# Two-layer decoder trunk on one core: the first weight tile loaded in two parts, and the blocks for the down-projection sums read ahead of two pooling weights

## The chip, the core and the metric

The kernel runs on one core of a Trainium2 chip. The metric is the device time of one execution in microseconds. The core has five engines with instruction streams of their own: TensorE (PE; weight loads show as PEld), VectorE (DVE), ScalarE (ACT), GpSimd (POOL) and SyncE (SP). SP does no arithmetic here: it issues most DMAs, in the order of its own program, and one that must wait holds up all that stand behind it. Engines tell each other of finished work by semaphores only.

## What is computed

Two layers over a stream x of 1024 positions by 1024 features, all in float32. Layer 0, cut to the parts that lie around the change:

```python
h = rms_norm(x, norm_gains[0, 0])
z = h @ w_in[0]                                  # 1024 x 1024
z_main, z_mem = z[..., :768], z[..., 768:]
y_main = pool_mixer(z_main, w_pool[0], pool_scale[0])   # causal means over 2/4/8/16 positions, then a product
y_mem = memory_attn(z_mem, mem, mem_norm[0], w_mem_kv[0])   # 4 heads over 256 memory rows
y = jnp.concatenate([y_main, y_mem], axis=-1) @ w_out[0]
x = x + rms_norm(y, norm_gains[0, 1])
h = rms_norm(x, norm_gains[0, 2])
gu = h @ w_gate_up[0]
y = (silu(gu[..., :2816]) * gu[..., 2816:]) @ w_down[0]
x = x + rms_norm(y, norm_gains[0, 3])
```

After layer 0 a shared K/V is projected; layer 1 has dilated attention in place of the pooling mixer and is otherwise built alike.

## The kernel before

**Tiling.** Features lie on the 128 partitions and positions along the free axis. A weight job is one 128-column tile of a weight matrix, 8 tiles of 128 x 128 (8 x 64 KB, 512 KB), or 3 of them (192 KB) for a pooling weight. Every float32 operand is split into a rounded high part and the rest as low part, and a product is three matmuls (high x high, high x low, low x high). For weights ACT makes the high part (WH from WR, `weight_hi`, L1076) and DVE or POOL the low part (WL, L1719 on DVE, L2599 on POOL). A job on 1024 positions is 6 matmuls of 512 columns for each of its k tiles.

**Start.** SP loads the constants (CN, 121 KB), the gains (GN, 47 KB), weight job 0, x tiles 0 to 3 (XS, 512 KB each, in two DMAs), weight job 1, x tiles 4 to 7. Of each x tile ACT makes the high part (XHA, L1234) and DVE the low part (XLA, `x0_low`, L1738). In between ACT and DVE split weight 0 (ahead of x tile 0) and weight 1 (ACT behind x tile 5, DVE behind x tile 6). PE runs job 0 ("in" tile 6) and waits before each k for `x0_lo`.

**Pooling stage (about 152 to 213 us).** Jobs 12 to 17 are the products with the pooling weights, in the order of POOL_OUT. In each job PE runs two attention steps of the memory heads in between. A step of PE is: PO (probabilities times values, L837), PTR (transpose of the probabilities, L847), PSC (scores, L865). A step of DVE is: maximum of the scores (MC, L1862), its negative (NM, L1868), and for the step before the reciprocal and scaling (RL L1881, PR L1882). ACT does the exponential (PR, L1191) and the copy of the transposed probabilities (PT, L1185). They hand over in a ring, so a wait of one holds all three. After the steps of job n ACT takes the product out of PSUM (YP, L1284) and splits coming weights: one for n = 0 and 1, two for n = 2 and 3, always the next ones in the list.

**Sums of the down-projection weights.** The down projection is a fast matrix product with 7 products, and needs sums of blocks of w_down. For each of 8 block sets c, SP reads two DMAs of 704 KB into ZS[c % 2] (`load_blocks`, L2773), DVE makes four sums in place (`weight_sums`, L1966 to L1970) and SP writes them back (`keep_blocks`, L2781). ZS[0] and ZS[1] lie on the memory of XLA, so set 0 may be read only when the last "in" job (job 11) is done. DVE makes the sums of set 0 around the two steps of pooling job 13 (n = 1; L1966 and L1967 ahead of the first step), those of sets 1 and 2 in n = 3 and 4, the others in the output projection.

**SP around this stage.** A weight may be read when the job that last used its slot is done. Slots go round in fours: the weight of job 15 waits for job 11, of job 16 for job 12, of job 17 for job 13. Output weights 0 to 3 (called out 0 to out 3 here; WR4 to WR7) lie on the memory of XS, and are free. SP's order is: weights 15, 16, 17, out 0 to out 3, block sets 0 and 1, then for each set: write it back, and read the one after next once this write has landed.

Of the kernel before, what the change touches and what calls it, by code (L numbers as in the profile page):

```python
# [10 lines left out]
ALU = mybir.AluOpType  # L11
# [3 lines left out]
P = 128  # L15
# [285 lines left out]
def build(nc, w_all, w_st, w_dn, x_t, mem_t, pos, gains, consts, masks, x_mid, inner, mem_keep, rstd_keep,  # L301
          trig_keep, w_keep, s_keep, t_keep, out_t):
    with ExitStack() as ctx:
# [210 lines left out]
        consts_in, tables_in = sem("consts_in"), sem("tables_in")  # L514
# [166 lines left out]

        px_order = {"PE": [], "ACT": []}
# [5 lines left out]
        def _(pe):  # L688
# [9 lines left out]
            def begin(j):  # L698

                pe.wait_ge(*lo_ready(j))  # L700
                for s, v in dict.fromkeys(PS_WAIT[j].values()):
                    pe.wait_ge(named[s], v)
# [175 lines left out]
            pe.wait_ge(consts_in, 32)  # L878

            xh, xl = xs(0)  # L880
            job(J[("in", 0, 6, None)], xh, xl, wait_k=lambda k: pe.wait_ge(x0_lo, k + 1))
# [182 lines left out]
        def _(act):  # L1064
# [164 lines left out]
            act.wait_ge(consts_in, 32)  # L1229
            A(NM[:, :], CN[:, 0:2], ACT.Copy)  # L1230
            weight_hi(0)
            for k in range(KT):
                act.wait_ge(x_in[k], 32)
                A(XHA[:, :, k, :], XS[:, k, :].rearrange("p (h c) -> p h c", h=2), ACT.Copy,  # L1234
                  scale=GN[:, k:k + 1]).then_inc(x0_hi, 1)
                if k == 5:
                    weight_hi(1)
            weight_hi(2)
# [464 lines left out]
        def _(dve):  # L1703
# [195 lines left out]
            dve.wait_ge(consts_in, 32)  # L1899
            weight_lo(J[("in", 0, 6, None)])  # L1900
            for k in range(KT):
                x0_low(k)
                if k == 6:
                    weight_lo(J[("in", 0, 7, None)])
            for k in range(1, KT):
                accumulate0(k)
            memory_low()
# [669 lines left out]
        def _(pool):  # L2577
# [32 lines left out]
            pool.wait_ge(consts_in, 32)  # L2610
# [84 lines left out]
        def _(sp):  # L2695
            loaded = [0]

            def load(j):
# [22 lines left out]
                sp.dma_start(raw(j), src.rearrange("p (k n) -> p k n", k=o.kn)).then_inc(s, 16)  # L2721
# [142 lines left out]
            def sub_layer(l):  # L2864

                if l == 0:
                    loads_to(J[("out", 0, 4, 0)])
                    sp.wait_ge(mm_done, J[("in", 0, POOL_IN[-1], None)] + 1)
                    load_blocks(0, 0)
                    load_blocks(0, 1)  # L2870
                    for c in range(8):
# [40 lines left out]
            sp.dma_start(CN[:, :], consts).then_inc(consts_in, 16)  # L2912
            sp.dma_start(GN[:, :], gains).then_inc(consts_in, 16)
            loads_to(1)
            for k in range(KT):
                if k == 4:
                    loads_to(2)
# [10 lines left out]
            loads_to(J[("out", 0, 0, 0)])  # L2928
# [139 lines left out]
```

## Time and profile before

| | us |
|---|---|
| Median of 3 runs | 2176.41 |
| Lowest and highest of them | 2172.22, 2179.36 |
| The profiled execution's own time | 2175.9 |
| Its span, first to last instruction | 2174.1 |
| PE busy | 2080.0 (96%) |
| DVE, ACT, POOL busy | 1474.5, 955.0, 338.2 |
| DMA, mean over the span | 164 GB/s |

The span is cut by what PE does: its busy time is 96% of it. The rest, 94 us, is made of waits, most of them shorter than 3 us. Busy times of matmuls are modelled, so starts are better read than ends. Times of a row count from the start of the span.

### The profile page before, as it was taken

To read this page: it belongs to the slowest core of one execution; us is meant where nothing else is said; L and a number is where in the kernel's file an instruction comes from. 1 tells how busy PE (TensorE), PEld (TensorE's weight loads), DVE (VectorE), ACT (ScalarE), POOL (GpSimd) and SP (SyncE) were. 2 spreads that over 40 slices of the span, in tenths; PEclk is the share of its full clock that TensorE was granted. 3 is DMA by queue.
4 is the path that set the end of the run, shared out by engine and by line. 5 is a ranking of instruction groups with operands and counts; after the bars stand their busy time and mean duration, and the time that the engine had idled before them with its cause. 6 is when DMAs were issued, how large, how long until landed. Compare 5 with 4: busy or idle time off the path is not lost.

```text
span 2174.1 us, 25430 instructions
## 1 busy us (share of the span) xinstructions
PE 2080.0 (96%) x9458; PEld 1676.4 (77%) x9458; DVE 1474.5 (68%) x2079; ACT 955.0 (44%) x1513; POOL 338.2 (16%) x188
## 2 busy tenths in 40 slices
PE   7995899999999999999999998999999999999997
PEld 6774788788888888887777776678788888877886
DVE  5555678477788875575455466467969998885665
ACT  6333354355554354343445556665622222234441
POOL 3632200021121000000000023020033333310001
PEclk9998999999999999999999999899999999999998
DMA  4206842355678876574111100113236654477554
GB/s 168 93 15 223 296 157 83 117 180 225 232 271 303 307 275 218 193 281 160 59 59 59 59 30 30 39 54 117 82 134 219 245 206 158 172 266 259 191 185 154
DMA packets 119755, 357.37 MB, mean 164 GB/s; under 512 B 10832, under 2 KB 12112, under 8 KB 114384
## 3 DMA queue, kind: packets, MB, share of 16 engines
q1 hardware_dynamic: 103168, 325.59, 42.0%
q10 hardware_dynamic: 16464, 30.15, 4.0%
q8 instruction: 75, 1.23, 0.2%
q14 instruction: 48, 0.39, 0.1%
HBM read 241.28 MB, written 114.43 MB: 164 GB/s over the span
## 4 chain that ended last, share of the span: by engine, by line
PE 73%; DVE 9%; DMA 7%; ACT 5%; issue 4%; SPq 1%; POOL 0%; ACTq 0%; POOLq 0%; DVEq 0%
PE PS L941 10%; PE PS L943 10%; PE PS L942 10%; PE PS L716 7%; PE PS L721 7%; PE PS L717 6%; PE PS L959 5%; PE PS L960 5%; PE PS L961 5%; PE PSC L865 3%; PE PO L837 2%; PE PTR L847 1%; DMA TP<-x_mid 1%; DVE SS L1754 1%; DMA inner<-TP 1%
## 5 line engine op out<-in xcount | busy, mean ns | idle before, releaser
L959 PE MATMUL PS<-RP,DH 128*128 128x512 f32 x616 | 241.0, 391 | 5.1 <-DVE RP L2181 5.1
L960 PE MATMUL PS<-RP,DH 128*128 128x512 f32 x616 | 239.8, 389 | 0.0
L961 PE MATMUL PS<-RP,DL 128*128 128x512 f32 x616 | 239.8, 389 | 0.0
L941 PE MATMUL PS<-BHT,SH 128*128 128x512 f32 x576 | 224.1, 389 | 0.0
L942 PE MATMUL PS<-BLT,SH 128*128 128x512 f32 x576 | 224.1, 389 | 0.0
L943 PE MATMUL PS<-BHT,SL 128*128 128x512 f32 x576 | 224.1, 389 | 0.0
L941 PE MATMUL PS<-BH,SH 128*128 128x512 f32 x432 | 168.2, 389 | 0.7 <-DVE SL L2082 0.7
L943 PE MATMUL PS<-BH,SL 128*128 128x512 f32 x432 | 168.1, 389 | 0.0
L942 PE MATMUL PS<-BL,SH 128*128 128x512 f32 x432 | 168.0, 389 | 0.0
L959 PEld LDWEIGHTS PS<-RP,DH 128*128 128x128 f32 x616 | 115.6, 188 | 31.4 <-DVE RP L2181 7.5
L1076 ACT ACTIVATE DH<-DR 128x1408 fp32r<-128x1408 f32 x56 | 77.3, 1380 | 135.5 <-DMA DR<-s_keep 88.5
L961 PEld LDWEIGHTS PS<-RP,DL 128*128 128x128 f32 x616 | 115.6, 188 | 24.3
L960 PEld LDWEIGHTS PS<-RP,DH 128*128 128x128 f32 x616 | 115.7, 188 | 23.5
L716 PE MATMUL PS<-XH,WH 128*128 128x512 f32 x320 | 132.4, 414 | 0.8 <-ACT TP L1604 0.4
L1191 ACT ACTIVATE PR<-PSC,NM 128x256 f32<-128x256 f32 (+1 forms) x144 | 63.4, 440 | 145.2 <-DVE NM L1868 144.8
L1335 ACT ACTIVATE SH<-SR 128x2048 fp32r<-128x2048 f32 x36 | 69.1, 1920 | 130.5 <-POOL SR L2680 94.4
L717 PE MATMUL PS<-XL,WH 128*128 128x512 f32 x320 | 126.0, 394 | 0.0
L943 PEld LDWEIGHTS PS<-BHT,SL 128*128 128x128 f32 x576 | 108.1, 188 | 22.6
L942 PEld LDWEIGHTS PS<-BLT,SH 128*128 128x128 f32 x576 | 108.1, 188 | 22.4
L941 PEld LDWEIGHTS PS<-BHT,SH 128*128 128x128 f32 x576 | 108.1, 188 | 22.3
L2645 POOL TENSOR_TENSOR VL<-VR,VH 128x1024 fp32r<-128x1024 f32 x24 | 58.2, 2423 | 416.1 <-ACT VH L1218 416.1
L1719 DVE TENSOR_TENSOR DL<-DR,DH 128x1408 fp32r<-128x1408 f32 x56 | 90.5, 1621 | 40.4 <-ACT DH L1076 40.3
(327 smaller groups left out, 4830.0 us busy)
## 6 DMA issues: line engine op xcount, KB each, us to landing
SR<-in_wst SPq DMA_DIRECT2D x36, 1024.0 KB, 4.8
ZS<-in_wdn SPq DMA_DIRECT2D x32, 704.0 KB, 5.8
s_keep<-ZS SPq DMA_DIRECT2D x32, 704.0 KB, 4.7
DR<-s_keep SPq DMA_DIRECT2D x32, 704.0 KB, 5.2
WR<-in_w SPq DMA_DIRECT2D x36, 512.0 KB, 4.8
inner<-TP SPq DMA_DIRECT2D x36, 512.0 KB, 4.4
DR<-in_wdn SPq DMA_DIRECT2D x24, 704.0 KB, 5.4
RR<-t_keep SPq DMA_DIRECT2D x16, 1024.0 KB, 5.2
```

Source lines behind the costliest of these rows:

```text
L716: MM(out[h], wh[:, i, :], rh(h, k), start=(i == 0), stop=False)
L717: MM(out[h], wh[:, i, :], rl(h, k), start=False, stop=False)
L721: ins = MM(out[h], wl[:, i, :], rh(h, k), start=False, stop=last)
L941: MM(BANK[bank], SH[b][:, w, c], BH[t][:, k, :], start=(k == 0), stop=False)
L942: MM(BANK[bank], SH[b][:, w, c], BL[t][:, k, :], start=False, stop=False)
L943: ins = MM(BANK[bank], SL[b][:, w, c], BH[t][:, k, :], start=False, stop=(k == 3))
L959: MM(bank, wh[:, i, :], rh, start=(i == 0), stop=False)
L960: MM(bank, wh[:, i, :], rl, start=False, stop=False)
L961: ins = MM(bank, wl[:, i, :], rh, start=False, stop=(i == KD - 1))
L1076: A(hi(j), raw(j), ACT.Copy).then_inc(w_hi, 1)
L1335: A(SH[pair_slot(q)][:, S3:, :], SR[pair_slot(q)][:, S3:, :], ACT.Copy).then_inc(st_hi, 1)
L1719: V.tensor_tensor(lo(j), raw(j), as_f32(hi(j)), ALU.subtract).then_inc(w_lo_dve, 1)
```

## The change

Two edits, both in layer 0.

1. **Start.** SP loads the gains first, then the first two k tiles of weight 0 (128 KB), x tile 0, the other six k tiles (384 KB), x tiles 1 to 3, then the constants, weight 1 and x tiles 4 to 7. ACT and DVE split weight 0 in two parts, around x tile 0. PE waits for the first part at k = 0 and for the second at k = 2. The waits for the constants are moved behind this on all engines.
2. **Block sets.** After the weight of job 15 SP waits for job 11 and reads sets 0 and 1; then weight 16, write-back of set 0, weight 17, read of set 2, and only then out 0 to out 3. From the write-back of set 1 on its order is as before.

No arithmetic is added; splitting weight 0 makes one DMA, one ACT and one DVE instruction more.

```diff
 PE
             def begin(j):
-                pe.wait_ge(*lo_ready(j))
+                if j:
+                    pe.wait_ge(*lo_ready(j))
...
-            pe.wait_ge(consts_in, 32)
+            def first_ready(k):
+                if k == 0:
+                    pe.wait_ge(first_lo, 1)
+                elif k == K0:
+                    pe.wait_ge(*lo_ready(0))
+                pe.wait_ge(x0_lo, k + 1)
...
-            job(J[("in", 0, 6, None)], xh, xl, wait_k=lambda k: pe.wait_ge(x0_lo, k + 1))
+            job(J[("in", 0, 6, None)], xh, xl, wait_k=first_ready)
+            pe.wait_ge(consts_in, 16)
 ACT
-            act.wait_ge(consts_in, 32)
-            A(NM[:, :], CN[:, 0:2], ACT.Copy)
-            weight_hi(0)
+            act.wait_ge(gains_in, 16)
+            A(NM[:, :], GN[:, 0:2], ACT.Copy)
+            act.wait_ge(first_in, 16)
+            A(hi(0)[:, 0:K0, :], raw(0)[:, 0:K0, :], ACT.Copy).then_inc(first_hi, 1)
+            hi_next[0] += 1
             for k in range(KT):
+                if k == 1:
+                    act.wait_ge(*load_seen(0))
+                    A(hi(0)[:, K0:, :], raw(0)[:, K0:, :], ACT.Copy).then_inc(w_hi, 1)
...
+            act.wait_ge(consts_in, 16)
             weight_hi(2)
 DVE
-            dve.wait_ge(consts_in, 32)
-            weight_lo(J[("in", 0, 6, None)])
+            dve.wait_ge(gains_in, 16)
+            dve.wait_ge(first_hi, 1)
+            V.tensor_tensor(lo(0)[:, 0:K0, :], raw(0)[:, 0:K0, :], as_f32(hi(0)[:, 0:K0, :]),
+                            ALU.subtract).then_inc(first_lo, 1)
+            lo_next[0] += 1
             for k in range(KT):
+                if k == 1:
+                    dve.wait_ge(w_hi, 1)
+                    V.tensor_tensor(lo(0)[:, K0:, :], raw(0)[:, K0:, :], as_f32(hi(0)[:, K0:, :]),
+                                    ALU.subtract).then_inc(w_lo_dve, 1)
                 x0_low(k)
...
             for k in range(1, KT):
                 accumulate0(k)
+            dve.wait_ge(consts_in, 16)
 SP
                 if l == 0:
                     loads_to(J[("out", 0, 4, 0)])
-                    sp.wait_ge(mm_done, J[("in", 0, POOL_IN[-1], None)] + 1)
-                    load_blocks(0, 0)
-                    load_blocks(0, 1)
-                    for c in range(8):
+                    for c in range(1, 8):
                         keep_blocks(0, c)
...
-            sp.dma_start(CN[:, :], consts).then_inc(consts_in, 16)
-            sp.dma_start(GN[:, :], gains).then_inc(consts_in, 16)
-            loads_to(1)
+            sp.dma_start(GN[:, :], gains).then_inc(gains_in, 16)
+            sp.dma_start(raw(0)[:, 0:K0, :], w_all[ROW["in", 0, 6], :, 0:K0 * P].rearrange("p (k n) -> p k n", k=K0)) \
+                .then_inc(first_in, 16)
             for k in range(KT):
+                if k == 1:
+                    loads_to(1)
                 if k == 4:
+                    sp.dma_start(CN[:, :], consts).then_inc(consts_in, 16)
                     loads_to(2)
...
-            loads_to(J[("out", 0, 0, 0)])
+            loads_to(J[("pool", 0, POOL_OUT[4], None)])
+            sp.wait_ge(mm_done, J[("in", 0, POOL_IN[-1], None)] + 1)
+            load_blocks(0, 0)
+            load_blocks(0, 1)
+            load(J[("pool", 0, POOL_OUT[4], None)])
+            keep_blocks(0, 0)
+            load(J[("pool", 0, POOL_OUT[5], None)])
+            load_blocks(0, 2)
             sp.wait_ge(x0_lo, KT)
             sub_layer(0)
```

`load` with j = 0 leaves out the first K0 = 2 k tiles, and POOL waits for `gains_in` and `consts_in` in place of the one count.

SP's order in the pooling stage before. WR3, WR0 and WR1 with 384 columns are the weights of jobs 15, 16 and 17, WR4 to WR7 are out 0 to out 3, ZS0 and ZS1 the block sets (x2: two DMAs):

```order
L2721 DMA WR3_116<-in_w 128x384
L2721 DMA WR0_113<-in_w 128x384
L2721 DMA WR1_114<-in_w 128x384
L2721 DMA WR4_117<-in_w 128x1024
L2721 DMA WR5_118<-in_w 128x1024
L2721 DMA WR6_119<-in_w 128x1024
L2721 DMA WR7_120<-in_w 128x1024
L2773 DMA ZS0_253<-in_wdn 128x2x704 x2
L2773 DMA ZS1_254<-in_wdn 128x2x704 x2
L2781 DMA s_keep<-ZS0_253 128x2x704 x2
L2773 DMA ZS0_253<-in_wdn 128x2x704 x2
```

And SP's order there now (L2749 is the weight load, L2801 the block read, L2809 the write-back):

```order
L2749 DMA WR3_116<-in_w 128x384
L2801 DMA ZS0_253<-in_wdn 128x2x704 x2
L2801 DMA ZS1_254<-in_wdn 128x2x704 x2
L2749 DMA WR0_113<-in_w 128x384
L2809 DMA s_keep<-ZS0_253 128x2x704 x2
L2749 DMA WR1_114<-in_w 128x384
L2801 DMA ZS0_253<-in_wdn 128x2x704 x2
L2749 DMA WR4_117<-in_w 128x1024
L2749 DMA WR5_118<-in_w 128x1024
L2749 DMA WR6_119<-in_w 128x1024
L2749 DMA WR7_120<-in_w 128x1024
L2809 DMA s_keep<-ZS1_254 128x2x704 x2
```

Sets 0 and 1 moved ahead of six weights; out 0 to out 3 moved behind the write-back of set 0 and the read of set 2.

SP's order at the start before:

```order
L2912 DMA CN_106<-in_consts 128x242
L2913 DMA GN_105<-in_gains 128x94
L2721 DMA WR0_113<-in_w 128x1024
L2919 DMA XS_70<-in_x 128x512 x8
L2721 DMA WR1_114<-in_w 128x1024
L2919 DMA XS_70<-in_x 128x512 x8
```

And now:

```order
L2937 DMA GN_105<-in_gains 128x94
L2938 DMA WR0_113<-in_w 128x256
L2947 DMA XS_70<-in_x 128x512 x2
L2749 DMA WR0_113<-in_w 128x768
L2947 DMA XS_70<-in_x 128x512 x6
L2944 DMA CN_106<-in_consts 128x242
L2749 DMA WR1_114<-in_w 128x1024
L2947 DMA XS_70<-in_x 128x512 x8
```

The same tensors stand ahead of x tile 4 in both; only their order differs.

## Rows read from the trace of the kernel before

**Rows 1.** PE's waits in 0 to 340: total us, times, longest us

```profile
PE PSC L865 <- ACT PR L1191: 17.2, 4, 14.8
PE PS L716 <- DVE XLA L1738: 10.2, 2, 10.0
PE PX L744 <- DVE SS L1754: 7.8, 1, 7.8
```

**Rows 2.** Chain that ended last, 161 to 210: start us, us, what

```profile
165.80 0.33 SPq L2721
...
168.07 0.91 SPq L2773
169.02 9.02 DMA ZS<-in_wdn
178.07 0.90 DVE ZS L1966
...
183.36 0.43 DVE MC L1862
...
193.21 1.03 ACT WH L1076
...
208.24 0.43 PE PS L911
```

**Rows 3.** Timeline of SP, 100 to 240: start us, us, DMA issues

```profile
152.85 4.59 SPq L2721 DMA_DIRECT2D WR<-in_w  x2
...
183.47 0.90 SPq L2781 DMA_DIRECT2D s_keep<-ZS  x2
188.57 1.21 SPq L2773 DMA_DIRECT2D ZS<-in_wdn  x2
...
210.68 0.89 SPq L2781 DMA_DIRECT2D s_keep<-ZS  x2
219.39 1.21 SPq L2773 DMA_DIRECT2D ZS<-in_wdn  x2
```

**Rows 4.** Timeline of PE, pooling stage; in brackets the idle before and its releaser

```profile
181.19 1.22 PE L865 MATMUL PSC<-KM,QF 64*128 64x256 f32 x2 [14.75 <-ACT PR L1191]
...
195.35 0.71 PE L837 MATMUL PO<-PT,VM 128*128 128x128 f32 x4 [0.23 <-ACT PT L1185]
...
207.12 0.69 PE L847 MATMUL PTR<-CN,PR 128*128 128x128 f32 x2 [4.09 <-DVE PR L1882]
```

**Rows 5.** Timelines of DVE (first two rows) and ACT, pooling stage and behind it

```profile
161.55 0.35 DVE L1882 TENSOR_SCALAR PR<-PR,RL 128x256 f32<-128x256 f32 x1
...
200.24 3.08 DVE L1970 TENSOR_TENSOR ZS<-ZS 128x704 f32<-128x704 f32 x1
...
180.57 0.47 ACT L1191 ACTIVATE PR<-PSC,NM 128x256 f32<-128x256 f32 x1 [17.09 <-DVE NM L1868]
...
227.03 1.06 ACT L1076 ACTIVATE WH<-WR 128x1024 fp32r<-128x1024 f32 x1 [3.22 <-DMA WR<-in_w]
```

**Rows 6.** Timeline of POOL: low parts of weights

```profile
162.81 1.02 POOL L2599 TENSOR_TENSOR WL<-WR,WH 128x384 fp32r<-128x384 f32 x1 [1.49 <-ACT WH L1076]
...
200.18 5.34 POOL L2599 TENSOR_TENSOR WL<-WR,WH 128x1024 fp32r<-128x1024 f32 x2 [3.45 <-ACT WH L1076]
```

**Rows 7.** Stages: us, busy PE, PEld, DVE, ACT, POOL (xcount), PEclk, DMA share, GB/s

```profile
166.40:181.20 14.80, 0.05 (x2) 0.02 (x1) 2.40 (x5) 0.63 (x3) 0.00 (x0) 0.68 0.92 350
...
203.00:216.70 13.70, 7.61 (x25) 5.96 (x24) 9.90 (x11) 6.27 (x9) 2.52 (x1) 0.75 0.77 273
216.70:262.00 45.30, 45.18 (x198) 37.08 (x198) 31.31 (x30) 16.26 (x27) 14.15 (x5) 1.00 0.83 296
```

**Rows 8.** Chain that ended last, start of the kernel; the last row is PE's timeline

```profile
8.17 7.20 DMA XS<-in_x
...
20.99 1.21 DVE XLA L1738
...
22.24 0.50 PE L716 MATMUL PS<-XHA,WH 128*128 128x512 f32 x1 [0.25 <-DVE XLA L1738]
```

More of the change, by code:

```diff
@@ L513, in build @@
         sums_in, sums_made, sums_kept = sem("sums_in"), sem("sums_made"), sem("sums_kept")
-        consts_in, tables_in = sem("consts_in"), sem("tables_in")
+        gains_in, consts_in, tables_in = sem("gains_in"), sem("consts_in"), sem("tables_in")
+        first_in, first_hi, first_lo = sem("first_in"), sem("first_hi"), sem("first_lo")
         mem_moved = sem("mem_moved")
@@ L680, in x_last @@
             return x_back[k // 4], 16 * (back_count(4, max(n for n in range(KT) if n % XDEPTH == k // 4)) + 1)
+        K0 = 2
         px_order = {"PE": [], "ACT": []}
@@ L2608, in weights_to @@
                     done[0] += 1
-            pool.wait_ge(consts_in, 32)
+            pool.wait_ge(gains_in, 16)
+            pool.wait_ge(consts_in, 16)
             for i in range(3):
@@ L2720, in load @@
                     return
-                sp.dma_start(raw(j), src.rearrange("p (k n) -> p k n", k=o.kn)).then_inc(s, 16)
+                k0 = 0 if j else K0
+                sp.dma_start(raw(j)[:, k0:, :], src.rearrange("p (k n) -> p k n", k=o.kn)[:, k0:, :]).then_inc(s, 16)
             def load_kept(i):
```

## The prediction

> **What bounds the kernel now.** I read the page first (PE is busy 96% of the span), so a gain has to come out of the 94 us in which PE waits. The list of PE's waits for the first 340 us [rows 1] shows the three largest of layer 0: 14.8 us in one piece for the exponential, 10.0 us at the very start for the low part of x tile 0, 7.8 us for the sums of squares. The change touches the places of the first two. The chain of waits [rows 2] says what is behind the 14.8: the weight of job 17 is issued at 165.80, when job 13 lets go of its slot, four output weights follow, the first block read is issued at 168.07, its last bytes arrive at 178.07, and only then does DVE run the sums that stand ahead of its attention step. ACT, which needs that step's maximum, starts its exponential at 180.57 after 17.09 us of idle [rows 5], and PE its scores at 181.19 after 14.75 us [rows 4]. DVE had been done with everything else at 161.55 + 0.35 = 161.90 [rows 5]. So DVE waits on a queue, not on work. The stage row shows that the queue is busy there, 350 GB/s for 14.8 us = 5.2 MB [rows 7], which is the 0.2 + 2.1 MB of weights and the 2.9 MB of two block sets: the sets wait behind the weights.
>
> **Edit 2, what it takes away.** Job 11 is done at 152.85, when the weight of job 15 is issued (the first of the two in that row) [rows 3]. The blocks come right behind it: four issues in about 3 us from 153.2. For their landing the nearest row is the one of before, 10.0 us from issue to use with 2.3 MB ahead of it on the queue [rows 2]; now 0.2 MB is ahead. One set is 1.44 MB, at 350 GB/s 4.1 us, and with some 2 us around it I expect set 0 to be in at about 159.5. Even with the full 10 us it would be 163.2. DVE wants it at 161.90, so the wait goes wholly, or to 1.3 us at worst.
>
> What is late next? DVE may start L1966 at 161.90 instead of 178.07, 16.2 us sooner. PE is free at 181.19 - 14.75 = 166.44 [rows 4], and its scores then take until about 167.1. The second maximum of this stretch, 183.36 before [rows 2], comes 5.3 us after the start of L1966, at 167.2: PE and DVE meet within 0.1 us. Against it stands POOL, which starts a 1.02 us subtraction at 162.81 [rows 6], in the middle of the sums, where before DVE was idle. That such a pair costs is seen in L1970 at 200.24, 3.08 us long beside POOL's 200.18 [rows 5, 6], where its fellows take 0.90 [rows 2]. So the stretch comes forward by 16.2 us at best and by 16.2 - 1.0 = 15.2 with POOL's op in its way. I take **15.2 us**, by the row of 200.24. The Trainium skill (SBUF — State Buffer, the section on two separate sides) calls the port pair of DVE and GpSimd an exclusive lock, held for the whole instruction: the trace agrees with it (a 0.9 us op became 3.08), and by the rule the loss here is the whole 1.0 us, which is what I take; without it the sum would be 1.0 us better.
>
> **Edit 2, what it adds.** SP now issues out 0 only behind the write-back of set 0 and the read of set 2. I work this out on the clock of before; the shift of 15.2 moves all of it alike. The write-back is issued at 183.47 as DVE ends the sums; it has landed 5.10 us later, when the next read is issued at 188.57 [rows 3]. From a block read to the use of the weight behind it one pair of rows shows 219.39 to 227.03, 7.64 us [rows 3, 5], the same four transfers in the same order. So out 0 can be used at 183.47 + 5.10 + 7.64 = 196.21. ACT wants it at 193.21, in job 14's list of two weights [rows 2]: a new wait of 3.0 us on ACT. At 219.39 the queue was not empty (it had been running full until then, with x tiles from ACT's queue), so 3.0 is rather an upper value; with 1.44 + 0.52 MB at 350 GB/s = 5.6 us and 1 to 1.5 us around it the wait is 2.0 to 2.5 us. I take **2.6 us**. The Trainium skill (DMA: Bandwidth & Descriptors, the section on the anatomy of one DMA) gives 2.0 us plus bytes over 436 GB/s; by it, as an estimate, the two transfers take 6.5 us and the wait would be 1.9. Behind the waiting ACT instruction are queued the copy of OF, PT and the next exponential; PE waited for that PT already (0.23 us, at 195.35 [rows 4]), so PE loses all of it, and DVE with it. Out 1 to out 3 land 1.5 us apart behind out 0 (0.52 MB each at 350 GB/s), and are wanted 6 us behind it and later (POOL takes the first of them at 200.18 [rows 6]): no further wait. Weight 16, issued at 157.1 as before but behind the sets, is in by 164 and wanted after 171; weight 17, behind the write-back, is in by 174 and wanted at 177.
>
> **The clock.** The granted clock was 0.68 in the 14.8 us of idle and 0.75 in the stretch of the 4.09 us wait at 207.12 [rows 4, 7]; one matmul then took 0.43 us from start to start [rows 2], where in the stage at 1.00 it is 45.18 / 198 = 0.23 [rows 7], so the levels are 1.2 and 2.4 GHz. The slow matmuls behind 181.19 cost little now, since DVE sets the pace there, and their end gives nothing beyond the 15.2. Behind the new gap of 2.6 + 0.23 us the clock may fall or not; PO, PTR and PSC of that step lie on the path behind it, short pieces of which PSC took 1.22 us at the low level at 181.19. At half the rate the three would take some 0.9 us more, so the price is between 0 and 0.9. I take **0.3**.
>
> **Edit 1.** PE starts earlier: the x tile 0 has 0.38 MB of weight 0 and 0.12 MB of constants less ahead of it, together 0.5 MB, at 350 GB/s about 1.4 us. But this gets used up: PE's last k waits for the low part of x tile 7. The chain [rows 8] goes from the landing of x tile 5 (8.17 + 7.20 = 15.37) through three ACT and three DVE instructions to 22.20, and PE starts at 22.24 after 0.25 us of idle. PE had caught up already. What stands ahead of x tile 5 on the queue is the same set of bytes in both orders, and the one extra issue of about 0.45 us is covered, since the tile takes 7.20 us to land after its issue. So PE starts about 1.4 us sooner, waits that much more at later tiles, and comes to job 1 at the same time. Cost and gain: 0, between -0.5 and +0.4 us. The extra instructions of ACT and DVE lie at x tile 1, well ahead of tile 5, at whose landing this chain begins.
>
> **Everything behind it.** The 4.09 us wait at 207.12 (DVE's sums of set 1 beside POOL) and the 7.8 us for the sums of squares hang on chains that start in the stage itself, set by set, with SP's order unchanged from the write-back of set 1 on. They move as a block: 0, within 1 us either way.
>
> **Sum.** 15.2 - 2.6 - 0.3 = 12.3 us. The profiled execution took 2175.9 us itself (1.8 us outside its span), 0.5 below the median of the runs. 2175.9 - 12.3 = **2163.6 us**, 0.6% faster. About 0.3% (6.5 us) is what a measurement of this kernel can tell from no change.
>
> **Rivals.** (A) The new wait hardly shows: the queue is faster and POOL's op slips beside the sums. 16.2 us gained, 2159.7. For it: the estimates of the queue are all below 3.0. Against: they would have to be below by another 2. (B) The new wait is much longer. The write-back of set 2 took 8.71 us, not 5.10, from 210.68 to the next read at 219.39 [rows 3], since other transfers were under way. Then out 0 comes at 199.8, ACT waits 6.6 us, PE's clock falls: 15.2 - 6.6 - 0.9 = 7.7 gained, 2168.2. Against it: in the new order only weight 17 is under way at that time. (C) The change doesn't do what it says: sets 0 and 1 land no sooner for DVE's purpose, because what held them is not the order but the queue; then 14.75 us stay and the time is 2175.9. Against it: the queue carries almost nothing between 153 and 165. (D) Slower. The gap at 195 and the one at 207 come close behind one another, and the clock stays at the lower level into the output projection. Each matmul there costs 0.43 - 0.23 = 0.20 us more, so from 12.6 / 0.20 = 63 matmuls on (of the 198 of that stage [rows 7]) the change is slower; with all of them 40 us are lost, and it ends near 2203. Against it: before, the same two gaps were 14.75 and 4.09 us, and the output stage ran at 1.00.
>
> **How the numbers follow.** Forecast 0.64, A 0.14, B 0.14, C 0.03, D 0.05. The forecast and A are faster by over 0.3% (below 2169.9), and so is B for the most part: faster 0.88, within 0.3% 0.07 (C and the upper end of B), slower 0.05. The range has the forecast's own bounds (gain 16.2 + 0.4 - 1.0 down to 15.2 - 1.3 - 4.5 - 0.9), B, and the 3 us by which runs of this kernel lie off their median: 2157.5 to 2171. Outside are C, D and a little more, under 2 in 10.
>
> **What would show it.** Right: block reads issued at 153 to 156; the wait of 14.75 at PSC L865 gone; DVE's first sum near 162, one of its sums 1 us longer beside POOL; an idle of 2 to 3 us ahead of ACT's WH for out 0, with the releaser DMA WR, and PE waiting as long for PT; PE's first matmul near 8.6 and the first one of job 1 where it was, near 23.6. Wrong: ACT's wait under 1 us or over 5; a DVE wait for ZS at set 0 or 2; PE's first job ending at another time; a granted clock below 1 between the 204th and the 250th us.

## The result, and the profile after

The changed kernel took 2164.68 us (median of 4 runs, 2161.32 to 2165.14), beside 2176.11 us for the kernel before (2172.22 to 2179.36). The ratio is 0.9936, with a 95% interval of 0.9916 to 0.9956, so it is faster by some 0.6%. The forecast was 2163.6. Between the two profiled executions, on which the sum was made, 11.2 us were gained (2175.9 to 2164.74); the sum had said 12.3.

PE's waits in the first 330 us of the changed kernel (who waited for whom, us in total, times, longest), which answer to [rows 1]:

```profile
PE PX L749 <- DVE SS L1772: 12.0, 1, 12.0
PE PS L721 <- DVE XLA L1756: 9.2, 3, 8.1
PE PO L842 <- ACT PT L1197: 4.3, 2, 3.7
PE PTR L852 <- DVE PR L1900: 2.7, 2, 2.1
PE PSC L870 <- ACT PR L1203: 2.2, 2, 1.5
```

The 14.8 us at PSC are gone. In their place stands one new wait, PO for PT, 3.7 us. The start's wait is 8.1 us where it was 10.0, and the last of the old three has grown from 7.8 to 12.0 us. In this execution, then, not everything moved as a block; in a second one of the same kernel (experiment 4) that wait was 8.0 us.

SP's order, which answers to [rows 3], in the changed kernel's timeline:

```profile
154.67 2.99 SPq L2801 DMA_DIRECT2D ZS<-in_wdn  x4
158.56 0.33 SPq L2749 DMA_DIRECT2D WR<-in_w  x1
168.65 0.90 SPq L2809 DMA_DIRECT2D s_keep<-ZS  x2
169.59 0.99 SPq L2749 DMA_DIRECT2D WR<-in_w  x1
174.16 1.21 SPq L2801 DMA_DIRECT2D ZS<-in_wdn  x2
175.41 2.14 SPq L2749 DMA_DIRECT2D WR<-in_w  x4
192.51 0.89 SPq L2809 DMA_DIRECT2D s_keep<-ZS  x2
197.62 1.20 SPq L2801 DMA_DIRECT2D ZS<-in_wdn  x2
199.87 0.88 SPq L2809 DMA_DIRECT2D s_keep<-ZS  x2
209.95 1.20 SPq L2801 DMA_DIRECT2D ZS<-in_wdn  x2
...
215.04 0.89 SPq L2809 DMA_DIRECT2D s_keep<-ZS  x2
225.56 1.20 SPq L2801 DMA_DIRECT2D ZS<-in_wdn  x2
```

Sets 0 and 1 are read from 154.67 on; the sums of set 0 follow at 163.25, in DVE's timeline, without a wait:

```profile
162.99 0.35 DVE L1900 TENSOR_SCALAR PR<-PR,RL 128x256 f32<-128x256 f32 x1
163.25 0.89 DVE L1992 TENSOR_TENSOR ZS<-ZS 128x704 f32<-128x704 f32 x1
164.17 0.89 DVE L1993 TENSOR_TENSOR ZS<-ZS 128x704 f32<-128x704 f32 x1
```

POOL's low part of a weight lies right over them:

```profile
164.25 1.69 POOL L2625 TENSOR_TENSOR WL<-WR,WH 128x384 fp32r<-128x384 f32 x1 [1.49 <-ACT WH L1088]
```

The write-back of set 0 lands and set 2 is read at 174.16, and only then are out 0 to out 3 issued, at 175.41. ACT comes to out 0 before it is there; its timeline shows the new idle, and behind it PT, for which PE waits:

```profile
181.86 1.06 ACT L1088 ACTIVATE WH<-WR 128x1024 fp32r<-128x1024 f32 x1 [3.36 <-DMA WR<-in_w]
182.94 0.59 ACT L1186 ACTIVATE OF<-PO 64x512 f32<-64x512 f32 x1
183.56 0.39 ACT L1197 ACTIVATE PT<-PTR 128x256 f32<-128x256 f32 x1
```

PE's timeline has the two gaps of the stretch, the new one and what is left of the 4.09 us one of [rows 4]:

```profile
184.00 0.71 PE L842 MATMUL PO<-PT,VM 128*128 128x128 f32 x4 [3.70 <-ACT PT L1197]
...
196.31 0.44 PE L852 MATMUL PTR<-CN,PR 128*128 128x128 f32 x2 [2.14 <-DVE PR L1900]
```

Last, stages of the changed kernel by windows (us, busy time of PE, PEld, DVE, ACT, POOL, granted clock, DMA share, GB/s), against [rows 7]:

```profile
184.00:192.60 8.60, 8.60 (x28) 6.68 (x29) 7.38 (x9) 5.46 (x10) 4.59 (x3) 0.60 0.11 42
192.60:200.00 7.40, 5.26 (x28) 4.33 (x28) 7.26 (x8) 2.93 (x4) 2.12 (x1) 1.00 0.60 215
...
204.00:250.00 46.00, 44.67 (x197) 36.51 (x195) 32.20 (x29) 15.50 (x26) 14.70 (x5) 1.00 0.79 284
```

The granted clock was 0.60 on average over the 8.6 us behind the new gap. It didn't fall at once: in the first of them it was still 0.94, then 0.50 (1.2 GHz) between 185 and 191, and 1.00 (2.4 GHz) again from 192 on and from 204 to 250:

```profile
185.00:191.00 6.00, 6.00 (x17) 4.58 (x18) 5.25 (x7) 4.59 (x7) 1.99 (x2) 0.50 0.01 3
```

**Where the time went, point by point along the kernel.** The table below is worked out from the traces: the start of the same instruction in the kernel before and in another, and the difference (us, negative is earlier). It has every kernel measured for this document; they are introduced in the experiments.

```
                  job 0's    pooling  sums of  last max.  sums of  sums of
kernel            last x low job 12   set 0    of pool.   set 4    set 7
                  (20.90)    (159.23) (178.07) (196.94)   (231.09) (263.80) (905)     end
changed            +1.00      +1.44   -14.81   -10.83     -9.31    -7.52    -9.64   -11.14
changed, again     +0.77      +0.44   -15.81   -12.03    -11.85   -11.58   -10.87   -12.02
start only         +1.06      +0.86    +3.81    +3.81     +3.97    +3.88    +3.30    +2.97
blocks only        +0.35      +0.19   -16.06   -12.62    -11.67   -11.92   -14.03   -14.95
out 0 early        +1.09      +0.87   -15.38   -14.34    -13.66   -11.71   -12.19   -13.05
y first            +0.78      +0.43   -15.82   -11.31    -13.34    -9.08    -7.28    -9.19
best               +0.27      -0.04   -16.29   -15.24    -13.65   -12.02   -12.42   -14.27
best, const. late  -0.35      -0.53   -16.77   -16.79    -15.87   -16.14   -16.46   -18.85
the same, again    +0.19      +0.94   -15.31   -14.28    -12.79   -11.10   -11.42   -12.26
split, const. late +0.84      +0.70   -15.55   -15.56    -14.46   -13.81   -14.31   -16.47
x late             +0.36      +0.08   -16.16   -12.44    -12.41    -9.45   -11.13   -14.28
best, x late       -0.33      -0.59   -16.84   -15.30    -15.07   -14.63   -15.40   -14.46
```

Times in brackets are those of the instruction in the kernel before; the columns are the low part of x tile 7, DVE's first step of pooling job 12, the first sum of sets 0, 4 and 7, the last attention maximum of the pooling stage, an instruction at 905 us and the last instruction. Two executions of one kernel (the first two rows; "best, const. late" and its repeat) differ by 1.0 and 1.5 us at set 0, by 4.1 and 5.0 us at set 7 and by 0.9 and 6.6 us at the end, so one trace settles a step only where the same step is seen in many rows. Three such steps are there: from job 12 to set 0 (the gain), from set 0 to the last maximum (the new wait), and from there to set 4 and 7 (the output projection).

### The profile page after: what moved, and what is told of

Same layout as the page of the kernel before. It is cut to its first block, busy times and chain, and to the rows that moved or that the text cites. A ratio compares the mean times of both kernels' runs of the same rounds, so it can differ in the third digit from the quotient of the medians.

```text
span 2162.9 us, 25437 instructions
## 1 busy us (share of the span) xinstructions
PE 2080.7 (96%) x9458; PEld 1676.5 (78%) x9458; DVE 1476.1 (68%) x2080; ACT 956.1 (44%) x1514; POOL 340.5 (16%) x188
## 4 chain that ended last, share of the span: by engine, by line
PE 72%; DVE 9%; DMA 8%; ACT 4%; issue 4%; SPq 1%; POOL 0%; ACTq 0%; POOLq 0%; DVEq 0%
PE PS L953 10%; PE PS L955 10%; PE PS L954 10%; PE PS L721 7%; PE PS L726 7%; PE PS L722 6%; PE PS L971 4%; PE PS L973 4%; PE PS L972 4%; PE PSC L870 3%; PE PO L842 2%; DMA s_keep<-ZS 1%; DMA TP<-x_mid 1%; DMA WR<-in_w 1%; PE PTR L852 1%
```

## The experiments

**1. The two edits apart.** Start only is the changed kernel with SP's order of before in the pooling stage:

```diff
-                    for c in range(1, 8):
+                    sp.wait_ge(mm_done, J[("in", 0, POOL_IN[-1], None)] + 1)
+                    load_blocks(0, 0)
+                    load_blocks(0, 1)
+                    for c in range(8):
...
-            loads_to(J[("pool", 0, POOL_OUT[4], None)])
...
-            load_blocks(0, 2)
+            loads_to(J[("out", 0, 0, 0)])
```

> Edit 1 alone (first weight in two parts, constants later), the block reads in their old order. The trace of the changed kernel has PE's first matmul 1.9 us sooner and its first matmul of job 1 1.0 us later. Theory: this 1.0 us is edit 1's own and stays to the end: first matmul near 8.1 us, low part of x tile 7 starting near 21.9 (before 20.90), the pooling wait of 14.8 us unchanged, 1.0 us slower than before, 2177. Rival (the prediction's own term): PE reaches job 1 at the old time and the 1.0 us came from something else in that run, 2176.

Measured: 2177.27 us (10 runs), ratio 0.9995 [0.9983, 1.0008]. The low part of x tile 7 starts at 21.96, as the theory wanted. But the pooling wait did not stay at 14.8 us; it was 16.1, and set 0 is summed 3.81 us late, 2.95 more than job 12 began late. The windows show one reason, start only first, the kernel before second:

```profile
160.00:166.00 6.00, 5.89 (x20) 4.07 (x21) 1.94 (x6) 3.17 (x8) 3.09 (x4) 0.72 0.00 0
160.00:166.00 6.00, 6.00 (x30) 4.74 (x31) 1.20 (x5) 2.72 (x6) 2.27 (x4) 1.00 0.01 3
```

In this execution the granted clock fell to 0.72 there, PE lost another 1.6 us up to the end of job 13, and in the old order the load of weight 17, with all that stands behind it, waits for that job (it was issued at 168.26, 165.80 before). The other 1.3 us went between the first block read and the first sum (11.3 us, 10.0 before). Blocks only is the kernel before with edit 2 alone:

> Edit 2 alone (block sets 0 and 1 ahead of six weights), the start as before. Theory: the whole gain is edit 2's, and it is 1.0 us larger than that of both together: 2163.7, PE's wait of 14.8 us gone, ACT idle 3.4 us ahead of the high part of out 0, PE's wait for the sums of squares near 12 us where it was 7.8. Rival: the two edits need each other (the start shifts what shares the queue later), then this is slower than both together.

Measured: 2163.49 us, ratio 0.9934 [0.9915, 0.9953]. The whole gain is edit 2's. The 14.8 us are gone and ACT's new idle is 3.18 us, but PE's wait for the sums of squares was 8.1 us, not the expected 12. Edit 1 gives nothing, although PE starts 1.9 us earlier with it in the changed kernel (0.9 in start only). In the changed kernel's PE timeline, the first matmul and the first one that needs x tile 7:

```profile
8.06 0.77 PE L721 MATMUL PS<-XHA,WH 128*128 128x512 f32 x1 [8.06 <-DVE XLA L1756]
...
23.23 0.50 PE L721 MATMUL PS<-XHA,WH 128*128 128x512 f32 x1 [0.18 <-DVE XLA L1756]
```

The latter was at 22.24 before [rows 8]: a whole microsecond lost, where the prediction had 0. ACT's timeline shows it already at the landing of tiles:

```profile
8.05 0.84 ACT L1249 ACTIVATE WH<-WR 128x768 fp32r<-128x768 f32 x1 [1.46 <-DMA WR<-in_w]
...
15.02 1.15 ACT L1251 ACTIVATE XHA<-XS,GN 128x1024 fp32r<-128x1024 f32 x1 [1.81 <-DMA XS<-in_x]
```

The second is x tile 4, at 14.05 before. The same bytes stand ahead of it; they came 1 us later. The windows of two microseconds say when. The kernel before:

```profile
4.00:6.00 2.00, 0.00 (x0) 0.00 (x0) 0.00 (x0) 0.00 (x0) 0.00 (x0) 1.00 0.96 369
```

The changed kernel:

```profile
4.00:6.00 2.00, 0.00 (x0) 0.00 (x0) 0.35 (x1) 0.55 (x1) 0.00 (x0) 1.00 1.00 225
```

369 - 225 = 144 GB/s over 2 us are 0.29 MB, which at 369 GB/s is 0.8 us. The windows beside it don't change that: the changed kernel is ahead from 2 to 4 us (244 GB/s, 176 before) and behind from 6 to 8 us (313, 380 before), and over the first 8 us it has moved 0.28 MB less. The DMA engines are as busy as before from 4 to 6 us (share 1.00 and 0.96): they move less in the time. Why is not shown.

**2. The load of out 0 one place earlier.** This takes the new wait away: out 0 goes right behind weight 17, ahead of the read of set 2.

```diff
             load(J[("pool", 0, POOL_OUT[5], None)])
+            load(J[("out", 0, 0, 0)])
             load_blocks(0, 2)
```

> The changed kernel with one load moved: out 0 is issued right behind weight 17, ahead of the read of set 2. Theory A (the new ACT wait is on the path and its gain survives): ACT's idle of 3.36 us ahead of the high part of out 0 is under 0.5, the pooling stage ends 3 to 4 us sooner, the write-back of set 1 and all sets behind it come about 3 us sooner, total 3 us faster than the changed kernel, near 2161.5. Theory B (from there on the end is set by the traffic of the queue, not by when the stage ends): the stage ends 3 to 4 us sooner but PE's wait for the sums of squares grows from 12.0 to 15 us, total within 1 us of the changed kernel.

Measured: 2160.72 us (2159.47 to 2162.81), ratio 0.9923 [0.9904, 0.9941]. ACT's timeline has no idle there any more, the last pooling weight and out 0 stand in one row:

```profile
177.41 1.46 ACT L1088 ACTIVATE WH<-WR 128x384 fp32r<-128x384 f32 x2
```

But PE's wait for PTR, 2.1 us in the changed kernel, is back at the size it had before:

```profile
PE PTR L852 <- DVE PR L1900: 4.7, 2, 4.1
```

From set 0 to the last maximum this kernel loses 1.0 us where the changed one loses 4.0, so the step gained 3.0 us here. The 1.0 us left is no wait but the granted clock. Out 0 early, and then the kernel "split, const. late" of experiment 4, which has the same order there and loses nothing:

```profile
176.90:181.10 4.20, 4.20 (x15) 2.90 (x15) 0.88 (x4) 3.51 (x7) 3.10 (x2) 0.68 1.03 414
177.00:181.00 4.00, 3.77 (x20) 2.44 (x17) 1.32 (x4) 3.39 (x8) 3.16 (x2) 1.00 1.04 419
```

PSC took 1.22 us in the first and 0.70 in the second. The other traces with out 0 early bear this out. Those that lose 1.0 us on this step (out 0 early, best, and the second execution of best, const. late) were granted 0.67 to 0.69 there; those that lose nothing (split, const. late, and the first execution of best, const. late) 1.00. As one kernel stands on both sides, this is a matter of the execution. Y first and "best, x late" lost 1.5 us just behind the first sum of set 0, where they were granted 0.57 and 0.62 and the others with the new order 1.00. So the whole effect of the new wait, with its clock, is up to 4.0 us at the place. At the end of pooling this kernel keeps 3.5 us (-14.34 against -10.83), at the end 1.9; the rest goes in the output projection.

**3. Is it ACT or the queue that sets the pace of the output projection?** In the changed kernel ACT waits 7.31 us for out 4 (3.22 before [rows 5]):

```profile
217.79 1.06 ACT L1088 ACTIVATE WH<-WR 128x1024 fp32r<-128x1024 f32 x1 [7.31 <-DMA WR<-in_w]
```

Behind it stand ACT's copies and squares of finished outputs, on which DVE waits. This kernel puts them ahead of the weight:

```diff
                     for m in range(KT):
-                        if m < 5:
-                            weight_hi(SPLITS[hi_next[0]])
                         if m == 0:
+                            weight_hi(SPLITS[hi_next[0]])
                             act.wait_ge(c_lo, 19)
                         first_y(s_y, J[("out", 0, m, 0)], m, 0)
+                        if 0 < m < 5:
+                            weight_hi(SPLITS[hi_next[0]])
```

> The changed kernel with ACT's order in the output projection turned: for m = 1 to 4 the product and its square are taken out of PSUM before the next weight's high part is made. There ACT idled 7.31 us for out 4's transfer (3.22 before) with the squares queued behind it, and DVE's sums of set 4 behind those. Theory A: this in-order wait is what gives the gain back: sums of set 4 start near 217 in place of 221.8, PE's wait for the sums of squares falls from 12.0 to 6 to 8 us, total 4 to 5 us faster, near 2160. Theory B: the queue sets the pace (set 4's read and the four weights behind it land when they land, and so do sets 5 to 7): PE's wait stays within 1.5 us of 12, total within 1.5 us.

Measured: 2166.09 us (2162.18 to 2168.59), ratio 0.9945 [0.9924, 0.9965]. ACT's wait for out 4 is gone and set 4 is summed 1.5 to 4 us sooner (-13.34, against -11.85 and -9.31 in two executions of the changed kernel), but set 7 comes at -9.08, between their -11.58 and -7.52. DVE's waits from 203 to 262, in the changed kernel and then in this one:

```profile
DVE ZS L1992 <- DMA ZS<-in_wdn: 15.3, 2, 7.9
DVE SS L1772 <- ACT TP L1115: 4.4, 1, 4.4
DVE ZS L1993 <- DMA ZS<-in_wdn: 17.6, 3, 8.3
```

DVE was held by ACT once, for 4.4 us ahead of set 4. With that gone it waits for the block sets instead, which come from the queue. Theory A falls. Of B the time holds (1.4 us from the changed kernel's), while PE's wait for the sums of squares is 9.9 us, 2.1 below the 12.0.

**4. The changed kernel again, and three mixtures.** One trace of the changed kernel had lost 3.3 us from the last maximum to set 7. The same kernel once more:

> The changed kernel as it is, once more, beside the three others of this job. Theory (the out-projection stretch is bound by the queue): from the read of set 3 to the read of set 5 pass 26 to 28 us, as in the five traces so far (25.8 before, 27.9, 27.5, 26.9, 25.9), whatever PE did at the end of the pooling stage; total 2164.7 within 1.5. Rival: the 12.0 us of PE's wait for the sums of squares in its first trace is part of the change, and comes again within 1 us.

Measured: 2163.63 us, ratio 0.9923 [0.9902, 0.9943]. The new wait is there again (3.28 us), but now everything behind moves as a block: -12.03, -11.85, -11.58 and -12.02 at the end, just as the prediction had it. From the read of set 3 to that of set 5 pass 25.75 us (27.94 in the first trace), and PE's wait for the sums of squares is 8.0 us, so the rival falls. The loss in the output projection is a matter of the execution. Next, the start of before with both block edits (best), the same with the constants behind x tile 7 and weight 0 whole, and the split weight with the constants there:

```diff
                 if k == 4:
-                    sp.dma_start(CN[:, :], consts).then_inc(consts_in, 16)
                     loads_to(2)
                 for h in range(2):
                     sp.dma_start(XS[:, k, HALF[h]], x_t[:, k, HALF[h]]).then_inc(x_in[k], 16)
+            sp.dma_start(CN[:, :], consts).then_inc(consts_in, 16)
```

> The block sets moved as in the change, out 0 ahead of set 2, and the start of the kernel before (no edit 1). Theory: ACT's new wait (3.4 us) and edit 1's loss (0.5 to 1.0 us at job 1) are both gone, and both come through to the end: 3.5 us faster than the changed kernel, 2161. Rival: they are swallowed by the queue in the output projection, 2164.

Measured: 2162.17 us, ratio 0.9917 [0.9893, 0.9941]. It is 1.5 us below the changed kernel on the same chip, which leaves theory (2161) and rival (2164) both open.

> As the one above, but with the gains first, weight 0 whole ahead of x tile 0, and the constants behind x tile 7. Theory: 121 KB less ahead of x tile 5 are worth 0.3 us: low part of x tile 7 starts 0.3 us sooner than before (20.6), PE's job 1 too. If the constants' first DMA cost nothing before, because it ran while the queue was still empty, it stays at 20.9.

Measured: 2160.01 us (2157.01 to 2161.64), ratio 0.9909 [0.9884, 0.9933]. The low part of x tile 7 started at 20.55, near the 20.6 of the theory, but at 21.09 in the kernel's second trace (experiment 5).

> Weight 0 in two parts around x tile 0 as in the change, the constants behind x tile 7, out 0 ahead of set 2. It parts edit 1's loss: if the constants in front of weight 1 are the cause (121 KB, 0.3 us, and an issue), the low part of x tile 7 starts at 20.9 as before; if it is the split itself (small DMAs at the start, the queue not yet full), it starts at 21.5 or later still.

Measured: 2159.49 us (2156.88 to 2163.05), ratio 0.9905 [0.9882, 0.9927]. The times don't tell the three apart. The start does, over all runs. The low part of x tile 7 is late by 1.00, 0.77, 1.06, 1.09, 0.78, 0.84 and 0.36 us in the seven kernels that split weight 0 (mean 0.84), and by 0.35, 0.27, -0.35, 0.19 and -0.33 in the five others (mean 0.03). Where the constants stand makes some 0.4 us (+0.35 and +0.27 with them first, -0.35, +0.19 and -0.33 with them last), within the scatter of these numbers. So the split itself costs 0.8 us, and it gives nothing back. With weight 0 whole and the constants behind, the queue ran in the same window at

```profile
4.00:6.00 2.00, 0.00 (x0) 0.00 (x0) 0.11 (x1) 1.06 (x1) 0.00 (x0) 1.00 1.04 347
```

and with the split and the constants behind at 289:

```profile
4.00:6.00 2.00, 0.00 (x0) 0.00 (x0) 0.31 (x1) 0.66 (x1) 0.00 (x0) 1.00 0.98 289
```

**5. What takes time back in the output projection.** The traces fall into two groups. ACT issues three reloads of x tiles (TP from in_x, 0.8 MB) at the start of that stage, when pooling is over on PE. The table gives their first issue counted from that of the write-back of set 2 (us), how long that write-back took, from its issue to the next read, and the time from the read of set 3 to that of set 5.

```
kernel              reloads behind   write-back   read of set 3
                    write 2 by       of set 2     to that of set 5
before                3.85             8.71          25.84
start only            3.79             8.88          25.97
changed, again        4.03             8.55          25.75
y first               4.02             8.53          25.88
changed               1.33            10.09          27.94
blocks only           2.68             9.70          27.48
out 0 early           2.91             9.44          26.94
best                  2.91            10.17          28.00
best, const. late     2.60             9.69          27.62
the same, again       2.92            10.22          29.57
split, const. late    2.64             9.87          27.83
```

Where the reloads come 3.8 us or more behind, the write-back takes 8.5 to 8.9 us; at 2.9 or less, 9.4 to 10.2, and set 5 is read 27 to 29.6 us behind set 3 where it was 26. In the second group PE had run ahead of DVE's sums by 1 to 2.5 us. Another sign of this lead is where ACT takes the last pooling product out of PSUM (YP): 2.6 to 2.9 us behind the write-back of set 2 in the first group, 0.15 to 1.7 in the second. To see whether it is the reloads or PE's lead, these two kernels move the reloads to the last step of the stage:

```diff
-                for n in range(XDEPTH):
+                for n in range(XDEPTH if l else 0):
                     x_reload(r, n)
...
+                        if m == KT - 1:
+                            for n in range(XDEPTH):
+                                x_reload(r, n)
```

> The changed kernel, with one thing moved: ScalarE issues its three reloads of x tiles (TP<-in_x, 0.8 MB together) not at the start of the output projection (201.2 us in the changed kernel's first trace) but behind its seventh step, at about 249 us. Theory: in the changed kernel these reloads stand in the queues ahead of the write-back of blocks 2, which then takes 10.1 us (8.7 in the kernel before) and pushes the next reads back. Without them the write-back of blocks 2 takes at most 8.7 us, from the read of blocks 3 to that of blocks 5 at most 26.0 us (27.9 in the first trace, 25.8 before), and the sums of sets 5 and 6 and all behind them keep the 12 us by which set 2 is early: span some 1 to 2 us below the first trace's 2162.9, near the second one's 2162.0. Rival 1: the stretch belongs to the other transfers there (writes and reads of blocks, weights), the reloads only share it; the read of blocks 5 stays 27 to 28 us behind that of blocks 3. Rival 2: the reloads come too late where they are put, VectorE waits for x tiles when it adds the residual, and the kernel is 2 us or more slower than the changed one.

> The kernel of best_cn (block reads moved, the weight of out 0 read ahead of blocks 2, first weight whole, constants behind x tile 7) with the three x tile reloads moved as in xlate_after. Theory: here the reloads stood ahead of the write-back of blocks 2 too (9.7 us; blocks 3 to 5 in 27.6 us), so both fall to at most 8.7 and 26.0 us, and the end comes 1.5 to 2 us sooner than in best_cn: time about 2158, ratio to the kernel before 0.990. Rival 1: blocks 3 to 5 stay at 27 to 28 us and the time is best_cn's within 1 us. Rival 2: VectorE waits for x tiles at the residual, 2162 or more.

> The kernel of best_cn once more, beside the two others on one chip. Both theories: 2160 us within 2 us, ratio 0.989 to 0.992; write-back of blocks 2 some 9.7 us, blocks 3 to 5 in 27.6 us, as in its first trace. If these two numbers come out near 8.6 and 25.9 instead, they are chance from run to run and the theory on the reloads falls.

Measured: x late 2161.60 us, ratio 0.9938 [0.9926, 0.9950]; best, x late 2162.88 us, 0.9938 [0.9921, 0.9954]; the control 2161.11 us, 0.9933 [0.9920, 0.9946]. In the control the write-back took 10.22 us and the stretch from set 3 to set 5 29.57, so the long values of its first trace (9.69 and 27.62) were not chance. SP's timeline of the control, write-back of set 2 and read of set 4:

```profile
196.39 0.88 SPq L2792 DMA_DIRECT2D s_keep<-ZS  x2
206.61 1.21 SPq L2784 DMA_DIRECT2D ZS<-in_wdn  x2
```

And with the reloads moved, first in best, x late, then in x late:

```profile
195.37 0.88 SPq L2795 DMA_DIRECT2D s_keep<-ZS  x2
203.72 1.21 SPq L2787 DMA_DIRECT2D ZS<-in_wdn  x2
...
198.27 1.06 SPq L2812 DMA_DIRECT2D s_keep<-ZS  x2
207.02 1.20 SPq L2804 DMA_DIRECT2D ZS<-in_wdn  x2
```

The write-back takes 8.35 us in place of 10.22 in the first pair, and 8.75 in place of 10.09 in the second. (The expectations call the reloads ahead of this write-back; the table shows that they are issued 1.3 to 4 us behind it.) Only the second pair says what the reloads do. In best, x late PE had no lead, as its YP shows, 2.9 us behind the write-back like in the first group:

```profile
198.28 1.12 ACT L1292 ACTIVATE YP<-PS,GN 128x1024 f32<-128x1024 f32 x1 [1.73 <-PE PS L920]
```

So its 8.35 us belong beside the 8.53 to 8.88 of that group, and not beside the control's 10.22. X late has the changed kernel's lead in full (YP 0.15 us behind), and its write-back is 1.3 us shorter: beside a lead, the reloads lengthen it by 1.3 us in this one pair. From set 3 to set 5 it took 26.7 us in x late, over the 26.0 that the theory wanted: the read of set 5 came 9.28 us behind the write-back of set 3 (5.24 in best, x late, 5.92 before). So something that goes with the lead costs 0.7 us or so by itself; what it is stays open.

What the reloads cost in time is open too. By ratio neither kernel with late reloads was faster than its fellow. But the changed kernel was not run again on that chip; beside its two medians from other chips x late is 2 to 3 us faster, and so it is at the end of its trace (-14.28 against -11.14 and -12.02), most of it gained behind 905 us. From set 6 to set 7 it had fallen back from -11.17 to -9.45.

**What is left of the gain.** The five measurements with out 0 early and the reloads in place have ratios 0.9923, 0.9917, 0.9909, 0.9933 and 0.9905; the four with the new wait and the reloads in place have 0.9936, 0.9923, 0.9934 and 0.9945. The means, 0.9917 and 0.9935, are 4 us apart. Each ratio is uncertain by 3 to 5 us, so this is likely and not proven, and the two kernels with late reloads, one with the new wait and one without, have 0.9938 both. On one chip the two kernels "best, const. late" and "split, const. late" took 2160.0 and 2159.5 us and the changed kernel 2163.6. Both beat the kernel before beyond doubt.

## Why the prediction was right

**The wait behind the blocks (15.2): right in kind, 1.0 too small.** From the first step of job 12 to the sums of set 0 each of the 11 traces with the new order comes forward by 16.24 or 16.25 us: the best case of the two bounds. DVE wanted to start at 161.90 by the old clock and did so within 0.1 us: 163.25, less the 1.44 us by which this execution was late, is 161.81. The block reads were issued at 154.67, less the same 1.44 just the 153.2 foretold, and set 0 had 8.6 us to land. The term had been cut to 15.2 because of POOL's 1.02 us operation. The two did meet, but it was POOL's that grew, to 1.69 us, while DVE's sums stayed at 0.89. The row of 200.24, by which I chose, has a DVE operation of 3.08 us beside POOL; its counterpart is still there:

```profile
189.41 3.08 DVE L1996 TENSOR_TENSOR ZS<-ZS 128x704 f32<-128x704 f32 x1
189.35 2.38 POOL L2625 TENSOR_TENSOR WL<-WR,WH 128x1024 fp32r<-128x1024 f32 x1 [4.01 <-ACT WH L1088]
```

The starts tell the two cases apart. At 164.17 DVE began 0.08 us ahead of POOL (164.25), and POOL grew; at 189.35 POOL began 0.06 us ahead of DVE, and DVE grew, as it did at 200.18 and 200.24 before. The one that came second waited. The Trainium skill (SBUF — State Buffer, the section on two separate sides) says just this: whichever of the two starts first has the shared ports for its whole instruction, and the other is blocked, for a VectorE instruction that reads two tensors in SBUF beside a GpSimd one that reads SBUF, as here. The prediction took from it only that somebody loses 1.0 us, and gave the loss to DVE. By its own rows DVE's second sum was due at 161.90 + 0.92 = 162.82 and POOL's operation at 162.81 [rows 6], which is too close to say who comes first. I should have kept both ends and not taken one for the sum.

**The new wait (2.6): right in kind and place, 0.8 too small.** ACT's idle was 3.36 us, and 3.28, 3.18, 3.09 and 2.49 in the other executions that have it, with the releaser DMA WR as foretold; PE waited 3.70 for PT. The step that failed is the correction from 3.0 to 2.6: the working from the pair of rows 7.64 us apart gave 3.0, and the argument that an emptier queue would be quicker cut it down. By the rows from the block read at 174.16 to the use at 181.86 it took 7.70 us, just as when the queue was full. The unchanged reading of the row would have been within 0.4, and those 0.4 are the write-back of set 0, which took 5.50 us and not 5.10 with weight 17 beside it. By the Trainium skill (DMA: Bandwidth & Descriptors, the section on the anatomy of one DMA) it would have been 1.9 us, as an estimate; the section gives that fit for one transfer issued by GpSimd, and these are two issued by SP. The measurement is the other way, and decides.

**The clock (0.3): right within what can be seen.** PE was at 1.2 GHz from 185 to 191, and the PSC at 184.86 took 1.22 us, not 0.70. What the wait cost in position was 3.98 us from set 0 to the last maximum, 0.3 more than the 3.70 of PE's wait; in changed, again, blocks only and x late the same difference is 0.2, -0.1 and 0.3. What the prediction did not have is that the clock can fall in this stage without the new gap too, for 1.0 to 1.5 us (experiment 2).

**Edit 1 (0): 0.8 too good.** "The same set of bytes" was true, and not enough. It took for granted that the queue moves those bytes at the same rate in whatever pieces they are asked for. With weight 0 in two parts it moved 225 GB/s in the fifth and sixth microsecond, not 369, and x tile 7 came 0.8 us later on average (1.00 in the profiled execution). The bounds of -0.5 to +0.4 didn't reach that far.

**Everything behind (0, within 1 us): right in one execution, 3.3 us off in the other.** In the second execution it moved as a block, from -12.03 to -12.02. In the first it lost 3.3 us up to set 7 and had them back at the end (what gave them back is not shown), and the kernels in which PE has a lead lose 0.7 to 3.3 us there (y first, which has none, 2.2, so the lead is not all of it). The sentence that these chains "start in the stage itself, set by set, with SP's order unchanged" overlooked that ACT has a queue of its own: its three reloads hang on PE's progress, not on SP's order, and move against the write-backs. The one clean pair of runs shows that these reloads lengthen a write-back by 1.3 us.

**The sum.** In the profiled execution: 16.25 (sets) - 3.98 (new wait with its clock) - 1.44 (late at job 12; 1.00 of it was there at x tile 7, the rest is not explained) = 10.83 us at the end of pooling, and 11.2 us at the end. The forecast of 12.3 had the gain 1.0 too small, the wait with its clock 1.1 too small, and nothing for the start. The first two cancel. That the forecast came within 1.1 us is therefore luck in part: without the error on the sets it would have been 2 us too good.

**The rivals.** Of A, half came true: POOL's operation slipped and DVE's did not. A's other half, no visible wait, is what the kernel with out 0 early does: 2160.7 us, against 2159.7 worked out for it. B's mechanism, a write-back of 8.7 us ahead of out 0, did not come: set 0's took 168.65 to 174.16, 5.5 us. C fell with the 14.8 us. D fell with the granted clock of 1.00 from 204 to 250 us.

## What to carry to other kernels

When a load is moved ahead of others on an in-order queue, price the loads that it overtakes by the nearest pair of rows with the same transfers, and leave the number as it stands. Here one weight too many had been overtaken: asking which of the overtaken loads is wanted first, and issuing that one ahead, gave another 3 to 4 us at the place. List every queue that hangs on the moved engines, not only the one whose order is edited; and don't expect smaller first transfers to gain anything when the end of the stage hangs on the last of them; here they cost 0.8 us. Before two kernels are compared on one stage, look at the granted clock of both there: it moved the stage by 1.0 to 1.5 us, once between two executions of one kernel. And a change that moves several things (here the reloads, and by chance PE's lead) needs a sign for each of them in the trace before one gets the credit.

## What was not expected of the hardware

- One more and smaller DMA at the start cost throughput. Weight 0 as 128 KB and 384 KB around an x tile: 225 and 289 GB/s between 4 and 6 us in the two kernels with the split whose windows are shown, 369 and 347 in the two without (0.28 and 0.31 MB less over the first 8 us); the last x tile 0.8 us later on average.
- When DVE's sum and POOL's subtraction overlap, the one that starts second pays, and 0.1 us decides: at 164.25 POOL (1.02 to 1.69 us, in all eleven traces with the new order, with DVE at 0.89), at 189.41 DVE (0.89 to 3.08 us).
- A write-back of 1.4 MB took 5.1 us alone, 5.5 us with one 0.2 MB weight beside it, 8.4 to 8.9 us beside the output weights, and 9.4 to 10.2 us when 0.8 MB of reads on another queue came less than 3 us behind it; moving those reads away in the changed kernel gave 8.75.
- Behind a gap of 3.7 us in PE's stream the granted clock was 0.50 from 185 to 191, starting some 1 us after PE had gone on; then it was back at 1.00 although a gap of 2.14 us followed. In three traces with out 0 early it was 0.67 to 0.69 over 4.2 us of the same stage with no gap over 0.7 us in the 6 us ahead, and in two with the same gaps ahead it was 1.00; one kernel showed both.
